# Two-block transformer kernel, sparse attention stage: half the compressed-input units, the position embedding as a fifth group of the compression product, the compressed bias table read by DMA, gate products turned, and two heads in one compressed score

## What is computed

```python
q, k_c, v_c, k_s, v_s, k_w, v_w, g = split(h @ w_in)      # 16 heads, 4 groups of 4, width 64
gates = sigmoid(g).reshape(B, S, G, R, 3)
# compression: 15 overlapping blocks of 32 tokens at stride 16, for keys and for values
blocks = x[:, blk_idx] + pos_emb[None, None, :, None, :]
flat = moveaxis(blocks, 3, 2).reshape(B, n_cmp, G, 32 * 64)
kc = gelu(flat @ w1) @ w2                                 # w1: 2048 x 128, w2: 128 x 64
...
dist = pos[:, None] - cmp_end[None, :]                    # cmp_end = 16 n + 31
bias = tbl[t5_bucket(dist)]
s = einsum('bsgrd,bngd->bgrsn', q, kc) * scale + bias
p_cmp = softmax(where(valid, s, NEG)) * valid
o_cmp = einsum('bgrsn,bngd->bsgrd', p_cmp, vc)
...
o = gates[..., 0:1] * o_cmp + gates[..., 1:2] * o_sel + gates[..., 2:3] * o_win
return o.reshape(B, S, H * 64) @ w_o
```

## Time and profile before

| | us |
|---|---|
| median of 3 runs | 2043.84 |
| lowest, highest | 2041.53, 2045.69 |
| the profiled execution | 2047.32 |
| its span, first to last instruction | 2045.4 |

### The profile page before, as it was taken

The page is one execution under the profiler, slowest core; times in us unless marked ns, Lnnn a source line. Parts: engine busy times, 40 slices in busy tenths (PEclk is TensorE's granted clock), DMA queues, the critical chain, the costliest instruction groups (busy, mean ns, idle before and its releaser), DMA issues.

```text
span 2045.4 us, 29867 instructions
## 1 busy us (share of the span) xinstructions
PE 1863.1 (91%) x11568; PEld 1495.6 (73%) x11568; DVE 1303.7 (64%) x2378; ACT 907.0 (44%) x1865; POOL 305.9 (15%) x340
## 2 busy tenths in 40 slices
PE   7999999999999999999999988899997877778877
PEld 7999889999999999869999878797533322223222
DVE  5555785655655562686555765577587767676454
ACT  4444464444444441474444443543454443444333
POOL 1000101000100010000000100023343333333331
PEclk9999899999999997899999899899999999999999
DMA  7555426955555534205555243249999999999998
GB/s 274 186 186 178 128 77 141 305 186 186 161 186 187 185 114 166 83 22 166 186 186 186 83 144 104 83 165 375 387 422 421 421 422 422 421 421 421 422 421 323
DMA packets 96972, 488.35 MB, mean 239 GB/s; under 512 B 10640, under 2 KB 10896, under 8 KB 63808
## 3 DMA queue, kind: packets, MB, share of 16 engines
q0 software_dynamic: 38368, 274.74, 34.9%
q1 hardware_dynamic: 58464, 211.70, 30.9%
HBM read 482.21 MB, written 4.19 MB: 238 GB/s over the span
## 4 chain that ended last, share of the span: by engine, by line
PE 61%; DMA 12%; DVE 11%; issue 8%; POOL 4%; ACT 3%; another core or an unknown queue 0%; POOLq 0%; ACTq 0%; SPq 0%; DVEq 0%
PE PS L535 16%; PE PS L536 15%; PE PS L537 15%; PE PS L2025 3%; DMA WH<-uv,A 3%; DMA YL<-uv,A 3%; DMA YH<-uv,A 2%; DMA raw<-uv,A 2%; DVE WL L969 2%; PE PS L2046 2%; PE PS L1540 1%; DMA A<-uv,A 1%; DMA WL<-uv,A 1%; DVE XL L977 1%; DMA XF<-uv,A 1%
## 5 line engine op out<-in xcount | busy, mean ns | idle before, releaser
L969 DVE TENSOR_TENSOR WL<-raw,WH 128x1024 fp32r<-128x1024 f32 (+1 forms) x379 | 451.7, 1234 | 92.4 <-ACT WH L639 91.8
L535 PE MATMUL PS<-XH,WH 128*128 128x256 f32 x1632 | 474.1, 290 | 28.9 <-DVE WL L969 15.6
L536 PE MATMUL PS<-XL,WH 128*128 128x256 f32 x1632 | 466.3, 286 | 0.0
L537 PE MATMUL PS<-XH,WL 128*128 128x256 f32 x1632 | 466.2, 286 | 0.0
L639 ACT ACTIVATE WH<-raw 128x1024 fp32r<-128x1024 f32 (+1 forms) x379 | 375.0, 1040 | 68.4 <-PE PS L537 41.4
L535 PEld LDWEIGHTS PS<-XH,WH 128*128 128x128 f32 x1632 | 315.5, 193 | 37.8 <-issue 18.8
L536 PEld LDWEIGHTS PS<-XL,WH 128*128 128x128 f32 x1632 | 316.3, 194 | 0.2
L537 PEld LDWEIGHTS PS<-XH,WL 128*128 128x128 f32 x1632 | 315.7, 193 | 0.0
L912 ACT ACTIVATE A<-A,RTK 128x1 f32<-128x1 f32 x256 | 75.0, 293 | 297.8 <-DVE A L1511 296.2
L535 PE MATMUL PS<-GH,WH 128*128 128x256 f32 x704 | 198.1, 281 | 0.0
L536 PE MATMUL PS<-GL,WH 128*128 128x256 f32 x704 | 197.8, 281 | 0.0
(11 more groups left out here) (305 smaller groups left out, 3128.8 us busy)
## 6 DMA issues: line engine op xcount, KB each, us to landing
raw<-wst SPq DMA_DIRECT2D x388, 512.0 KB, 4.5
raw<-wst SPq DMA_DIRECT2D x9, 384.0 KB, 3.7
vscr<-A POOLq DMA_DIRECT2D x1, 3072.0 KB, 36.4
A<-vscr POOLq DMA_DIRECT2D x1, 2048.0 KB, 22.3
C<-cst SPq DMA_DIRECT2D x1, 1236.5 KB, 10.8
raw<-uv,A POOLq DMA_INDIRECT x65
hT<-xin SPq DMA_DIRECT2D x2, 512.0 KB, 4.7
A<-vscr POOLq DMA_DIRECT2D x1, 1024.0 KB, 12.0
```

The lines of the kernel that those rows point to most:

```text
L535: pe.matmul(o, wh, xh, start=start, stop=False, skip_group_check=True)
L536: pe.matmul(o, wh, xl, start=False, stop=False, skip_group_check=True)
L537: return pe.matmul(o, wl, xh, start=False, stop=stop, skip_group_check=True)
L969: dv.tensor_tensor(WL[:, m % SPL, 0:w], raw[:, i % RAW, 0:w], f32(WH[:, m % SPL, 0:w]), ALU.subtract).then_inc(s_lo, 1)
```

## The change

- `kc` and `vc`: two units each instead of four, with the columns of two groups side by side. VectorE reads each half of the partitions twice, across partitions for one of the two copies.
- The embedding becomes a fifth group of `KC2` (75 columns instead of 60); the matmuls of one column are gone. GpSimd zeroes and fills the fifth group ahead of w1.
- The compressed bias: one one-hot unit of 33 x 512 (256 KB, plain) behind `mla_o` instead of four in the stage; one product there, copied by VectorE, written 8-fold to DRAM (`cscr`) by GpSimd and read back as `BC` by two DMAs with rows of 15 numbers.
- Gates: weights (48 columns) as the stationary operand, 256 tokens as columns; ScalarE copies the product out, TensorE transposes it in two pieces behind `ks` 0, ScalarE applies the sigmoid.
- Compressed scores: `KCT` holds the keys of two groups in a block-diagonal pattern, so a matmul gives two heads (30 columns).
- Order: `nq` 5 moves ahead of the w2 product for values; VectorE reads `ks` 0 while ScalarE does the exponential; the transposes of `PC` go to banks 6 and 7 and wait for the reads of `ks` and `kw` instead of that of `vsw`.

```diff
+    add("ohc", 512, False, lambda a: onehot_cmp())
...
-    for g in range(4):
-        bt("kc", "nsa_w_in", 0, np.tile(1024 + 64 * g + ar(64), 2))
-    for g in range(4):
-        bt("vc", "nsa_w_in", 0, np.tile(1280 + 64 * g + ar(64), 2))
+    for t in range(2):
+        bt("kc", "nsa_w_in", 0, 1024 + 128 * t + ar(128))
+    for t in range(2):
+        bt("vc", "nsa_w_in", 0, 1280 + 128 * t + ar(128))
     for c in range(4):
...
         bt("nq", "nsa_w_in", 0, q[128 * (c + 4):128 * (c + 4) + 128])
-        add("ohc", 1024 if c < 3 else 768, False, lambda a, c=c: onehot_cmp()[:, c * 1024:(c + 1) * 1024])
...
+            po.dma_start(bass.AP(tensor=cscr.tensor, offset=0, ap=[[8 * 513, 16], [513, 8], [1, 512]]),
+                         flat(NST)[0:16, 384:896].unsqueeze(1).broadcast_to([16, 8, 512])).then_inc(s_cvs, 16)
...
+            po.wait_ge(s_cvs, 16)
+            for blk in range(2):
+                po.dma_start(BC[:, blk], bass.AP(tensor=cscr.tensor, offset=15 - 8 * blk, ap=[[32, 128], [8 * 513, 16], [1, 15]])
+                             ).then_inc(s_bc, 16)
...
+            po.wait_ge(s_gl, 3 * NF)
+            po.memset(KC2[0][:, 4, :], 0.0)
+            po.memset(KC2[1][:, 4, :], 0.0).then_inc(s_posz, 1)
+            po.wait_ge(s_posz, 1)
+            po.tensor_copy(KC2[0][:, 4, 0:32:2], c("pos", 0, 16))
+            po.tensor_copy(KC2[1][:, 4, 0:32:2], c("pos", 16, 32)).then_inc(s_pos, 1)
...
+            ac.activation(GTT, PS[0:48, 6, 0:T], ACT.Copy).then_inc(s_gtt, 1)
+            hi("ks", 0)
             ac.wait_ge(s_rtk, 1)
+            ac.wait_ge(s_gtr, 1)
             for blk in range(2):
-                ac.activation(GT[:, blk].rearrange("p s m -> p (s m)"), PS[:, 6, 48 * blk:48 * blk + 48], ACT.Sigmoid,
+                ac.activation(GT[:, blk].rearrange("p s m -> p (s m)"), PS[:, 5, 48 * blk:48 * blk + 48], ACT.Sigmoid,
                               scale=RTK[:, blk:blk + 1]).then_inc(s_gt, 1)
+            hi("ks", 1)
             ac.wait_ge(s_scs, 1)
             ac.activation(SCC, SCC, ACT.Exp).then_inc(s_sce, 1)
-            for t in range(2):
-                hi("ks", t)
             for t in range(2):
                 hi("kw", t)
...
-            dv.tensor_copy(NST[0:16, 0, 0:384], PS[0:16, 7, 0:384]).then_inc(s_tv, 1)
+            dv.wait_ge(s_plain, plain_n[where["ohc"][0]])
+            dv.tensor_copy(NST[0:16, 0, 0:384], PS[0:16, 7, 0:384])
+            dv.tensor_copy(flat(NST)[0:16, 384:896], PS[0:16, 5, 0:512]).then_inc(s_tv, 1)
...
+                dv.wait_ge(s_used, U(("kc", "vc")[kv], t))
+                for e in range(2):
+                    r = slice(64 * e, 64 * e + 64)
+                    dv.tensor_tensor(KC2[kv][0:64, 2 * t + e, :], PS[r, BANKS[n], 0:T], RT[r, 1, :], ALU.mult)
+                    ins = dv.tensor_tensor(KC2[kv][64:128, 2 * t + e, 0:255], PS[r, BANKS[n], 1:256], RT[r, 1, 1:256], ALU.mult)
...
-            dv.wait_ge(s_plain, 8)
...
             lo("ng", 0)
             own(dv.memset(PC[:, :, :], 0.0))
             dv.wait_ge(s_cs, 1)
-            dv.wait_ge(s_bc, 1)
+            dv.wait_ge(s_bc, 32)
...
+            dv.tensor_tensor(S3, S3, CS[:, 0].rearrange("p b s -> p (b s)").unsqueeze(2).broadcast_to([128, 32, 15]),
+                             ALU.subtract).then_inc(s_scs, 1)
...
+
+            dv.wait_ge(s_pad, 2)
+            ksw(0)
+            dv.wait_ge(s_sce, 1)
...
+            ins.then_inc(s_p3, 1)
+            for n in range(1, 4):
+                ksw(n)
...
+                    if n == NF:
+                        pe.wait_ge(s_tv, 1)
...
+            R, s, v = plain("ohc", 0)
+            pe.wait_ge(s, v)
+            pe.matmul(PS[0:16, 5, 0:512], c("rel")[0:33, :], R[0:33, 0:512], start=True, stop=True,
+                      skip_group_check=True).then_inc(s_plain, 1)
...
+                    pe.wait_ge(s_kc, 2 * kv + 2)
+                    pe.wait_ge(s_pos, 1)
+                    if kv:
+                        pe.wait_ge(s_rtk, 1)
...
-                        r = KC2[kv][:, :, 2 * lp:2 * lp + 225:16]
-                        w = R[:, 128 * i:128 * i + 128]
...
-                        ins = pe.matmul(PS[:, 2 + kv, 0:1], w, c("pos", 16 * kv + lp, 16 * kv + lp + 1), start=lp == 0,
-                                        stop=lp == 15, skip_group_check=True)
+                        ins = pe.matmul(PS[:, 4 + kv, 0:75].rearrange("p (a b) -> p a b", a=5), R[:, 128 * i:128 * i + 128],
+                                        KC2[kv][:, :, 2 * lp:2 * lp + 225:16], start=lp == 0, stop=lp == 15, skip_group_check=True)
                     ins.then_inc(s_plain, 1)
...
+            nq(5)
...
-                R, s, v = plain("ohc", n)
-                pe.wait_ge(s, v)
...
-                    ins = pe.matmul(PS[:, 4, 16 * k:16 * k + 16], R[0:33, 128 * (k % 8):128 * (k % 8) + 128], c("rel")[0:33, :],
...
-                ins.then_inc(s_plain, 1)
+            nq(6)
+            nq(7)
...
+            for kc in range(8):
+                w = slice(48 * kc, 48 * kc + 48)
+                ins = three(pe, PS[0:48, 6, 0:T], H[:, w], L[:, w], XH[:, kc, :], XL[:, kc, :], kc == 0, kc == 7)
+            ins.then_inc(s_used, 1)
+            pe.wait_ge(s_q, 8)
...
-                    for j in range(8):
-                        g = 2 * (j // 4) + e
...
+                for j in range(8):
+                    ins = pe.matmul(PS[:, 2, 240 * blk + 30 * j:240 * blk + 30 * j + 30], Q[:, j, 128 * blk:128 * blk + 128],
+                                    KCT[:, j // 4].rearrange("p e n -> p (e n)"), start=True, stop=True, skip_group_check=True)
             ins.then_inc(s_cs, 1)
             for n in range(4):
-                pe.wait_ge(*((s_q, 6 + n) if n < 3 else (s_gt, 2)))
+                pe.wait_ge(*((s_q, 6 + n) if n < 3 else (s_gtt, 1)))
                 gemm(("ks", "kw")[n // 2], n % 2, 0, 8, X, PS[:, (7, 0, 1, 6)[n], 0:T]).then_inc(s_used, 1)
-            pe.wait_ge(s_bc, 1)
-            pe.wait_ge(s_hid, 2)
+                if n == 0:
+                    pe.wait_ge(s_gtt, 1)
+                    for blk in range(2):
+                        ins = pe.transpose(PS[:, 5, 48 * blk:48 * blk + 48], GTT[:, 128 * blk:128 * blk + 128], c("ident")[0:48, 0:48])
+                    ins.then_inc(s_gtr, 1)
+            pe.wait_ge(s_gt, 2)
...
-            pe.wait_ge(s_vsw, 1)
+            pe.wait_ge(s_ksw, 4)
...
-                    ins = pe.transpose(PS[:, 4 + blk, 128 * i:128 * i + 128], PC[:, blk, 128 * i:128 * i + 128], c("ident"))
+                    ins = pe.transpose(PS[:, 6 + blk, 128 * i:128 * i + 128], PC[:, blk, 128 * i:128 * i + 128], c("ident"))
...
+                        pe.wait_ge(s_pcc, 2)
...
-                        pe.wait_ge(s_pcc, 2)
+                        pe.wait_ge(s_vsw, 1)
```

More of the change, by code:

```diff
@@ L160, in onehot_cmp @@
 def onehot_cmp():
[L161 to L162 removed]
+    r, s = np.arange(16)[:, None], np.arange(32)[None, :]
+    return onehot((16 * (15 - s) + r - 31).reshape(-1))
 def const_layout():
@@ L254, in wait, with program @@
         self.eng.wait_ge(self.sem, self.n if n is None else n)
-def program(nc, wst, cst, x, skt, uv, out, vscr, units):
+def program(nc, wst, cst, x, skt, uv, out, vscr, cscr, units):
     ctx = ExitStack()
@@ L771, in act_program @@
             prenorm(4)
-            for n in range(8):
-                hi("kc" if n < 4 else "vc", n % 4)
+            for n in range(4):
+                hi("kc" if n < 2 else "vc", n % 2)
                 if n == 0:
```

129 lines of the change are left out of this document (45 added, 84 removed).

## The result

The changed kernel takes **1994.76 us** (median of 4 runs, 1994.23 to 1995.34), the kernel before 2044.76 (4 runs, 2041.53 to 2046.28). The ratio is 0.9756, 95% interval 0.9740 to 0.9771. The forecast was 1999.0, with a range of 1993 to 2009: 50.0 us were saved where 44.8 were expected. The profiled execution took 1995.34 us, its span is 1993.5.

A forecast was written before the change was run, and what follows sets the result against it. The prediction took PE's own instruction stream to bound the stage. Terms of -49.1 in the stage, +2.3 at the FFN start and +2.0 for the weight stream made -44.8, from 2043.84 to 1999.0 us, range 1993 to 2009.

The forecast's parts named there:

- kc and vc: Compressed-input units in the stage: eight products of 2.85 us become four, -11.4 us.
- Embedding as a fifth group: w1 part of the stage: one-column matmuls go, 75 columns still cost 0.109 us a pass, -7.2 us.
- Bias table: Stage: four one-hot products go, 24.3 us become 12.2, -12.1 us, 7 of it passes and 5 half-clock products.
- Gates: Gates in the stage: 48 passes in 8.5 us become 24 matmuls of 256 columns in 2.85, -5.7 us.
- scores: Compressed scores in the stage: 64 passes in 12.9 us at half clock become 32 in 3.5 at full, -9.4 us.
- FFN start: First block's second FFN: GpSimd's squares, and PE's sums with them, end later, +2.3 us, bounds 1.1 to 4.
- Weight stream: Behind the bias table's 3 MB write: late weights stall PE, +2 us, between 0 and 8.
- Cover of 8 us: Stage: the exponential's chain lets VectorE's last k read end some 15 us after the scores; PE asks at 23.
- Rival 1: Clock falls behind the compressed scores and stays down, costing some 9 us: 2004 to 2009 us, chance 0.11.
- Rivals 2 and 4: Weight stream stalls PE, clock falls: 2004 to 2012, chance 0.11; small pieces block DMA engines: 2045 to 2070, chance 0.02.
- rival 3: Gates' chain exceeds its 8 us of cover and PE waits ahead of vsw: 2002 to 2012 us, chance 0.05.
- rival 5: More saved than counted: stream finds its gaps, 48-column products load faster, 1990 to 1994 us, chance 0.05.

The follow-up runs named there:

- a_again: The changed kernel profiled a second time, unaltered, in another session: 1998.60 us (5 runs), ratio 0.9754 to the kernel before.
- cover: Changed kernel with four copies of 768 columns on ScalarE ahead of the compressed scores' exponential: median 1999.12 us, ratio 0.9788.
- early_squares: Changed kernel with GpSimd's eight squares ahead of its table wait, DMA issues and memsets, TensorE waiting for VectorE's copies: median 1993.11 us, ratio 0.9750.
- flying4: Changed kernel with at most 4 gathers of expert rows in flight instead of 8: median 1991.90 us, ratio 0.9750.
- columns: Changed kernel with the four w1 halves over 75, 60, 30 and 15 columns, the left-out groups' products missing: stage 77.7 us.

## Why the forecast was right, and where it wasn't

The time fell where the forecast put it, in PE's own instructions of one stage. Term by term, first profiles, forecast and measured:

- kc and vc, -11.4: **-11.0**. Four products gone, and in this profile a fall of the clock beside the sums that is 6.8 us long instead of 3.4 (in a_again it is 3.4).
- Embedding as a fifth group, -7.2: **-5.9**. The part is 16.8 us, not 15.5, since a half takes 1.99, not 1.75, and a query product between them 2.95, not 2.85. The assumption that 75 columns cost what 60 do failed: 0.124 us a pass, above the 0.12 that the forecast had named as a sign of being wrong. It comes of how the columns lie; the row of 384 columns, on which one bound rested, streams them side by side. The other had been read too freely: 0.109 was the mean of unlike passes, since in the first profile of before the two passes of 60 columns take 0.27 us from start to start and the two of one column 0.18.
- Bias table, -12.1: **-12.0** (24.26 to 12.25). The sum holds; the share of 5 put down to the clock was real in that profile, but bringing the small products back doesn't bring it back.
- Gates -5.7, scores -9.4: **-5.7 and -9.4** (2.80 and 3.49 us). Each undone alone costs 7.0 and 7.8, not its term: a fall that one of them starts slows the rows behind it too.
- ks and kw -1.8: **-1.6**. vsw 0: **-0.1**. Transposes -1.5: **-1.5**, no wait at 805.46, and VectorE's read lies beside them.
- Sum -49.1: **-47.4**, and -52.0 in the second pair, since before itself varies. One profile was taken for a stage that varies by 5 us.
- FFN start, +2.3: **+1.4** (345.56 against 343.88, of which 0.29 were there at 333.4). The chain is as described; the term mis-sized is GpSimd's second issue, 0.57 us instead of 1.26: it is for 128 rows, and the row that its price was read from for 2048.
- Weight stream, +2: **0**. ScalarE waits, PE doesn't. The lower bound was right.
- The table reads: landed 22.7 and 23.5 us after their issue, at 402 us, ahead of the 430 foreseen; 24 was taken. Hidden, as said.
- Cover of 8 us at the gates' chain: **0.4** (cover). The forecast compared the end of the chain with the transposes, and missed that VectorE's split of the next weight unit is queued behind the wait for the exponential. It did no harm by luck.

Rival 1 exists in small: one fall behind the scores in a_again, where the first ks product takes 4.53 us instead of the 3.01 of after, 1.5 where 1.7 was foreseen, and a fall at the same place in early_squares and flying4 (3.4 us long) and in columns (6.8). It never stayed down. Rivals 2 and 4 are out, rival 3 stood 0.4 us away. The 1994.76 lie between rival 5 (1990 to 1994) and the forecast's own lower end, 1995 with no stall of the stream; that the stream finds its gaps, which rival 5 names, is part of it (the 2 us above), and faster 48-column products are not (2.80 us, 2.85 was taken).

From 44.8 to 50.0, with the means of the two profiles of each kernel: the way to the stage costs 2.1 us instead of 4.3 (2.2 of the difference); the stage gives 49.7 instead of 49.1 (0.6; the terms over-counted by 1.7 are made good by before's mean of 125.2 us, where the profile read had 122.5); the second block, whose instructions are the same, is 1.4 shorter by its falls of the clock; and the row "last sums to the first slot" is 3.5 shorter, since both profiles of before and one of the changed kernel have the late signals at the start of the expert layer. The two rows left take back 0.6. That makes 51.9, the difference of the spans. The profiled executions lie above the medians of their sessions, those of before by 2.3 us and those of the changed kernel by 0.6, which leads back to the 50 of the medians.

So the forecast missed by 5 us, and of these only 2.8 are in what it had counted. The rest, falls of the clock in unchanged code and the late signals, had no term in it, and that they went the changed kernel's way in these profiles is luck. The 2.1 us ahead of the stage stand firmer than two profiles let one think: from the first bias product (L1710, now L1733) to the stage's sums it takes 394.7 and 395.8 us before, and 396.6 to 398.2 in eleven profiles that have the change there. The later start of the FFN is 1.4 of it; the rest goes with falls of the clock at 531 us and just before the stage, which are there or not in either kernel.

## What to carry to other kernels

In a stage where one engine is busy in every row, a sum of its instructions forecasts well; take the clock's part from more than one execution, and don't tie it to the instruction beside which it falls, since the price appears one row further down. For the cover of a new wait, look not at the end of its chain but at the next thing queued behind it on the same engine that someone else needs. A stepped operand can have a price of its own: in unsplit fp32 passes 60 columns in steps of 16 elements cost no more than 15, but 75 did, where 105 side by side cost nothing more.
